# Both feed-forward products by Strassen's seven products, with the forms between them sent through HBM

## The chip, the cores and the metric

The kernel runs on one NeuronCore of one Trainium2 chip. Five engines take part: TensorE (PE, matmuls into the eight banks of PSUM), VectorE (DVE), ScalarE (ACT), GpSimd (POOL, here an issuer of DMAs and of a few memsets), and SyncE (SP, an issuer of DMAs). The metric is the device time of one execution in microseconds, the median over the runs. Lower is better.

## What is computed

A first block (attention with a stick-breaking weight, chunkwise retention, a gated merge) gives x. A second block mixes tokens with gated linear attention and sliding-window attention, and then has a feed-forward part. Only this last part is touched. Cut to what matters, with x of 1024 tokens by 1024 columns in float32:

```python
D_FF = 4 * D_MODEL                      # 4096
h = rmsnorm(x, norm_ff_w)               # 1024 x 1024
a = jnp.square(jax.nn.relu(h @ w_ff1))  # 1024 x 4096
x = x + a @ w_ff2                       # 1024 x 1024
out = rmsnorm(x, final_norm_w)
```

Every operand of a matmul is held as two fp32r values, hi and lo = value - hi, and a product is the sum of three: hi*hi, hi*lo and lo*hi. A block of 256 weight columns on all 1024 tokens and 1024 inner rows is thus 8 x 3 matmuls of 512 columns for each of its four outputs of 128 x 512.

## The kernel before

The stages follow one another: 30 projection blocks of the first layer, attention, retention, merge, the second layer's mixers, its output product (four blocks, L7), the norm before the feed-forward (`n3`), and then the feed-forward itself.

**Feed-forward.** It runs in four turns (`ff_turn`: line 1298 on ACT, 1889 on DVE, 2500 on PE; the last three PE turns, and the first three of ACT and DVE, are hardware loops). In each turn PE first makes four blocks of 256 hidden columns from `A_hi`, `A_lo` (line 450: weights stationary, 512 tokens moving), then four blocks of 256 output columns from the hidden values `F_hi`, `F_lo` of this turn (line 444: tokens stationary, 256 weight columns moving, two such strips in one bank). All go through `gemm` (line 431), which uses banks 0 to 3 in turn and waits for `kept[j]` before bank j is written again. SP loads one megabyte of weights for each block (`load_block`, 417) into one of two slots; ACT rounds it to hi (`split_hi`, line 425), DVE subtracts to get lo (`split_lo`, line 429). Hidden outputs are taken by ACT (relu, line 1305, then square into `F_hi`, line 1307) and by DVE (square again, 1896, minus hi, 1898). Outputs of the second product are added by DVE to the residual `X1` in place (line 1906), which stays in SBUF. The last norm (ACT 1319 to 1323, `final_scale` 1911 on DVE) goes by tiles of 128 tokens while the last block is made, and SP stores each tile.

**The norm before it.** `LateNorm` (313) is laid over the last block of the output product: for each of eight tiles of 128 tokens ACT makes the statistics (336 to 340), DVE scales (364), PE transposes eight squares into two banks (395), ACT rounds to `A_hi` (345), DVE makes `A_lo` (369). `pe_between` (398) puts the transpositions between outputs: tiles 6 and 7 come after output 0 of the first hidden block, and transposition t waits for the lo of tile t-1.

**The projections already have the seven products.** `product` (1948) makes one of seven products of a 2 x 2 split: 4 inner rows x 3 matmuls of 512 columns, in bank (7n + o) % 4; its bank is written again four products later, after `product_read` (576). DVE makes the four weight sums (`proj_sums`, 1349, 1355 to 1361), the lo parts (`proj_lo`, 1363, 1369) and seven additions that put the products together (`with_product`, 1413, 1415); ACT keeps product 0 (934) and rounds seven weight parts (865, 872). POOL stores four results of 256 KB in each block (756). The moving operands are parts of `A_hi`/`A_lo` for three products and of packed token sums `T_hi`/`T_lo` for four.

The order on every engine is the order of the program, written out by hand; there is no planner. DMAs of SP and POOL are issued in order in each queue, and a wait there holds back all that is behind it.

Of the kernel before, what the change touches and what calls it, by code (L numbers as in the profile page):

```python
# [5 lines left out]
SEQ, DM = 1024, 1024  # L6
# [59 lines left out]
def build(nc, x, norm_gain, w_in, b_merge, sb_q_gain, sb_k_gain, ret_out_gain, w_branch_sb, w_branch_ret, w_out,  # L66
# [152 lines left out]
    pos[0] = work_at  # L219
    F_hi = work("f_hi", [P, KT, SEQ], f32r)  # L220
    F_lo = work("f_lo", [P, KT, SEQ], f32r)
    FS = [work(f"fs{u}", [P, HALF]) for u in range(2)]

    YB = [at(f"yb{u}", [P, DM], off=a_at + u * DM * 4) for u in range(4)]
    GF = at("gf", [P, DM], off=a_at + 4 * DM * 4)

    ctx = ExitStack()
    with ctx:
# [18 lines left out]
        NPROJ = 30  # L247
        proj_d = nc.dram_tensor("projections", (NPROJ, P, 2 * SEQ), f32, kind="Internal").ap()
# [64 lines left out]
        class LateNorm:  # L313
# [3 lines left out]
            def __init__(self, name, eps, n, gain_at, meta_in=None):  # L317
# [4 lines left out]
            def parts(self, t):  # L322
# [4 lines left out]
                return (X1[:, t, :], XS[t % 4][:, :], stats[:, 16 + t:17 + t],  # L327
# [33 lines left out]
            def dve_scale(self, dve, t):  # L361
                src, scr, st, _, _ = self.parts(t)
                dve.wait_ge(self.rstd, self.m + t + 1)
                dve.scalar_tensor_tensor(scr, src, st, G1[0:src.shape[0], :], ALU.mult, ALU.mult).then_inc(self.scaled, 1)
# [38 lines left out]

        def level_keep(dve, p, v):
# [26 lines left out]
        def gemm(pe, n, s, hi, lo, rows_out, between=None, before=None, banks=range(4)):  # L431
# [72 lines left out]
        n2 = LateNorm("norm2", 1e-5, L6 - 1, 16, meta_in)  # L504
        n3 = LateNorm("norm3", 1e-5, L8 - 1, 32)
# [12 lines left out]
        f_hi = sem("hidden_hi")  # L518
# [71 lines left out]
        def tile_free(eng, n, j):  # L590
# [3 lines left out]
            elif before:  # L594
                eng.wait_ge(c_stored[out_tile(n, j)], stores_before(n, j))

        @block.sync
        def _(sp):
# [119 lines left out]
            with sp.Fori(0, 2) as i:  # L718
                for s in range(2):
                    load_block(sp, L7 + 2 * i + s, s, w7_d[:, :, ds(i * (2 * BC) + s * BC, BC)])  # L720
            f1_d = w_ff1_2[0].rearrange("(k p) c -> p k c", p=P)
            f2_d = w_ff2_2[0].rearrange("(g k p) c -> p g k c", p=P, k=KT)
            with sp.Fori(0, 4) as i:
                for s in range(4):
                    load_block(sp, L8 + 8 * i + s, s % 2, f1_d[:, :, ds(i * (4 * BC) + s * BC, BC)])
                for s in range(4):
                    load_block(sp, L8 + 8 * i + 4 + s, s % 2, f2_d[:, ds(i, 1), :, s * BC:(s + 1) * BC].rearrange("p g k c -> p (g k) c"))
# [1816 lines left out]
```

## Time and profile before

| | us |
|---|---|
| median of 3 runs (2843.64 to 2852.22) | 2848.79 |
| the profiled execution, its own time | 2846.42 |
| its span, first to last instruction | 2844.9 |
| PE busy in the span | 2714.9 |
| DVE / ACT busy | 1382.2 / 970.4 |
| POOL / mean DMA rate | 139.8 / 74 GB/s |
| mean granted TensorE clock | 0.973 of full |

Busy time of PE counts modelled ends of overlapping matmuls; the distance from one start to the next is the better measure of its pace. Idle time of an engine that nobody waits for costs nothing. The page's "L" numbers are lines of the kernel before.

### The profile page before, as it was taken

What the parts mean: (1) busy time and instruction counts of PE and PEld (TensorE: products, weight loads), DVE (VectorE), ACT (ScalarE), POOL (GpSimd) and SP (SyncE); (2) the same over time, 40 slices, a digit from 0 to 9 for tenths busy, and PEclk for the clock granted to TensorE, in tenths of its full rate; (3) what the DMA queues carried; (4) which work ended last, traced back from release to release, by engine and by line L of the source; (5) the groups of instructions that cost most, each with busy time, mean ns of one, the idle gap of its engine ahead of it and who ended that gap; (6) DMA issues with size and microseconds to landing.
All of it is one profiled execution on the core that took longest, in us unless ns stands there. A gap on an engine that the chain in (4) does not pass through costs nothing.

```text
span 2844.9 us, 36583 instructions
## 1 busy us (share of the span) xinstructions
PE 2714.9 (95%) x15024; PEld 2293.6 (81%) x15024; DVE 1382.2 (49%) x1818; ACT 970.4 (34%) x1587; POOL 139.8 (5%) x231
## 2 busy tenths in 40 slices
PE   5999999999999999999999899999999999999998
PEld 4777888887777778788897668877888989989888
DVE  7665556555565553656434571377343232232223
ACT  6444222334666553124123341243233021120221
POOL 0001111110000001000110000000100000000000
PEclk7999999999999999999999899898999999999999
DMA  2223333323202206342322001100221111111112
GB/s 98 89 92 112 97 115 97 111 102 120 82 28 82 74 26 228 106 163 67 114 86 104 16 1 45 45 16 1 89 64 49 45 45 45 46 45 46 52 53 82
DMA packets 129133, 211.67 MB, mean 74 GB/s; under 512 B 6205, under 2 KB 107242, under 8 KB 124762
## 3 DMA queue, kind: packets, MB, share of 16 engines
q1 hardware_dynamic: 110186, 147.16, 15.6%
q0 software_dynamic: 18800, 62.38, 6.2%
q8 instruction: 113, 1.85, 0.3%
q14 instruction: 34, 0.28, 0.0%
HBM read 163.38 MB, written 46.14 MB: 74 GB/s over the span
## 4 chain that ended last, share of the span: by engine, by line
PE 87%; DVE 5%; ACT 3%; issue 2%; DVEq 1%; ACTq 1%; DMA 1%; SPq 0%; POOL 0%; POOLq 0%
PE ps L450 23%; PE ps L1956 20%; PE ps L444 20%; PE ps L2055 4%; PE ps L2039 2%; PE ps L2012 2%; PE ps L2338 2%; PE ps L2405 2%; PE ps L2420 1%; PE ps L2218 1%; PE ps L1966 1%; PE ps L2023 1%; PE ps L2190 1%; DVEq L1492 1%; PE ps L2118 1%
## 5 line engine op out<-in xcount | busy, mean ns | idle before, releaser
L425 ACT ACTIVATE w_hi<-w_raw 128x2048 fp32r<-128x2048 f32 x60 | 114.8, 1914 | 554.5 <-DMA w_raw<-in_w_ff 363.1
L450 PE MATMUL ps<-a_hi,w_hi 128*128 128x512 f32 x736 | 295.4, 401 | 4.8 <-issue 3.5
L450 PE MATMUL ps<-a_lo,w_hi 128*128 128x512 f32 x736 | 292.9, 398 | 0.0
L450 PE MATMUL ps<-a_hi,w_lo 128*128 128x512 f32 x736 | 290.7, 395 | 0.0
L444 PE MATMUL ps<-w_lo,f_hi 128*128 128x256 f32 x1024 | 289.8, 283 | 0.0
L444 PE MATMUL ps<-w_hi,f_hi 128*128 128x256 f32 x1024 | 289.8, 283 | 0.0
L444 PE MATMUL ps<-w_hi,f_lo 128*128 128x256 f32 x1024 | 289.8, 283 | 0.0
L429 DVE TENSOR_TENSOR w_lo<-w_raw,w_hi 128x2048 fp32r<-128x2048 f32 x60 | 137.4, 2291 | 311.8 <-ACT w_hi L425 311.8
L1415 DVE TENSOR_TENSOR proj_out<-ps,proj_out 128x512 f32<-128x512 f32 x210 | 142.0, 689 | 237.7 <-PE ps L1956 237.7
L1956 PE MATMUL ps<-t_hi,pw_hi 128*128 128x512 f32 x480 | 196.4, 409 | 3.8 <-DVE t_lo L1389 3.8
L444 PEld LDWEIGHTS ps<-w_hi,f_hi 128*128 128x128 f32 x1024 | 196.6, 192 | 0.2
L444 PEld LDWEIGHTS ps<-w_lo,f_hi 128*128 128x128 f32 x1024 | 196.6, 192 | 0.2
L444 PEld LDWEIGHTS ps<-w_hi,f_lo 128*128 128x128 f32 x1024 | 196.6, 192 | 0.0
L1956 PE MATMUL ps<-t_lo,pw_hi 128*128 128x512 f32 x480 | 188.1, 392 | 0.0
L444 PE MATMUL ps<-w_hi,a_hi 128*128 128x256 f32 x640 | 181.5, 284 | 5.1 <-DVE a_lo L1815 5.1
L444 PE MATMUL ps<-w_lo,a_hi 128*128 128x256 f32 x640 | 181.4, 283 | 0.0
L444 PE MATMUL ps<-w_hi,a_lo 128*128 128x256 f32 x640 | 181.4, 283 | 0.0
L450 PEld LDWEIGHTS ps<-a_hi,w_hi 128*128 128x128 f32 x736 | 139.5, 190 | 40.9 <-issue 6.8
L450 PEld LDWEIGHTS ps<-a_lo,w_hi 128*128 128x128 f32 x736 | 139.2, 189 | 33.8 <-issue 2.2
L450 PEld LDWEIGHTS ps<-a_hi,w_lo 128*128 128x128 f32 x736 | 139.6, 190 | 31.8
L1956 PE MATMUL ps<-a_hi,pw_hi 128*128 128x512 f32 x360 | 150.9, 419 | 3.5 <-DVE a_lo L1347 3.5
L1956 PE MATMUL ps<-a_lo,pw_hi 128*128 128x512 f32 x360 | 144.1, 400 | 0.0
(365 smaller groups left out, 5688.0 us busy)
## 6 DMA issues: line engine op xcount, KB each, us to landing
w_raw<-in_w_ff SPq DMA_DIRECT2D x32, 1024.0 KB, 5.2
pw_raw<-in_w_in SPq DMA_DIRECT2D x30, 1024.0 KB, 5.4
projections<-proj_out POOLq DMA_DIRECT2D x88, 256.0 KB, 3.4
w_raw<-in_w_in SPq DMA_DIRECT2D x20, 1024.0 KB, 5.2
projections<-proj_sq POOLq DMA_DIRECT2D x32, 256.0 KB, 2.7
w_raw<-in_w_out SPq DMA_DIRECT2D x8, 1024.0 KB, 5.0
x_in<-in_x SPq DMA_DIRECT2D x8, 512.0 KB, 5.4
q<-projections SPq DMA_DIRECT2D x4, 1024.0 KB, 4.8
```

Of the source, the lines that this page charges most:

```text
L425: act.activation(W_hi[s][:, :, :], W_raw[s][:, :, :], ACT.Copy).then_inc(w_hi, 1)
L429: dve.tensor_tensor(W_lo[s][:, :, :], W_raw[s][:, :, :], W_hi[s][:, :, :].bitcast(f32), ALU.subtract).then_inc(w_lo, 1)
L444: last = pe.matmul(bank[banks[j]][:, r * BC:(r + 1) * BC], a[:, k, t:t + P], w[s][:, k, :], start=(k == 0 and g == 0), stop=(k == KT - 1 a ...
L450: last = pe.matmul(bank[banks[j]][:, :], w[s][:, k, ct * P:(ct + 1) * P], a[:, k, t0 + th * HALF:t0 + (th + 1) * HALF], start=(k == 0 and ...
L1415: return dve.tensor_tensor(PC[out_tile(n, j)][:, :], product_bank(n, o), src, ALU.add)
L1492: dve.drain()
L1956: last = pe.matmul(product_bank(n, o), w, a[:, k0 + k, t], start=(k == 0 and g == 0), stop=(k == 3 and g == 2))
L2012: pe.matmul(z, Q[:, c, qt * P:(qt + 1) * P], K[:, c, h:e], start=True, stop=(e < w))
L2039: last = pe.matmul(bank[2][:, lo:2 * P], V[:, kb, c * P:(c + 1) * P], WT[c][:, kb, lo:2 * P], start=(kb == 0), stop=(kb == qt))
L2055: last = pe.matmul(bank[3], w[b][:, k, ct * P:(ct + 1) * P], a[:, k, META + th * HALF:META + (th + 1) * HALF], start=(r == 0), stop=(r == ...
L2338: last = pe.matmul(bank[7][:, 0:2 * P], a, b, start=(m == 0), stop=(m == len(ops) - 1))
L2405: last = pe.matmul(bank[2 * (U % 3) + t // 4][:, (t % 4) * P:(t % 4 + 1) * P], a, b, start=True, stop=True)
```

## The change

**First product.** Hidden block 0 stays a plain `gemm` with its own weight tiles (`FD_hi`, the second projection weight slot). Hidden blocks 1 to 15 become blocks `NPROJ` to `NPROJ + 14` of the projection scheme: seven products each, with `proj_sums`, `proj_lo`, `with_product` as they are. The token sums are new: ACT copies the first half of the tokens out once more (`F_FIRST`), DVE makes the sums, partly inside the norm, from PSUM (`TokenSumNorm`).

**Between the products.** ACT applies relu and square in place to the four tiles of a block. DVE makes three sums and one difference of them (`hidden_sums`, one block later). POOL stores the seven forms (`a11 a22 a12 s1 s3 s2 s4`, 256 KB each) in HBM, 28 MB in all. `X1` is stored too (4 MB) and its space reused.

**Second product.** Four groups of 1024 hidden rows, seven products in each, 28 products. A product reads one form (1 MB, `hidden_form` on SP, ring of three) and one weight form made from quarters of 1 MB (`weight_quarter`, 16 in all, ring of five). It is four row outputs of 128 tokens x 512 columns: 4 x 4 x 3 matmuls of 512 columns, in one half of PSUM, the other half being read. For each, ACT rounds both forms (128 x 2048 each), DVE makes a weight sum in four of seven (`weight_sum`), both lo parts, and adds the four banks to an accumulator (`keep_product`). The residual is loaded into three accumulators and one spare quarter. Late products gather the accumulators into `Y`, tokens 512 to 1023 first, and the last norm runs on these tiles in the order 4 5 6 7 0 1 2 3.

The core of the diff:

```diff
+        class TokenSumNorm(LateNorm):
+            def act_hi(self, act, t):
...
+                last = act.activation(A_hi[:, :, c], turned, ACT.Copy)
+                if t < 4:
+                    act.activation(F_FIRST[0][:, :, t * P:(t + 1) * P], turned[:, 0:4, :], ACT.Copy)
+                    last = act.activation(F_FIRST[1][:, :, t * P:(t + 1) * P], turned[:, 4:8, :], ACT.Copy)
+                last.then_inc(self.hi, 1)
+            def dve_lo(self, dve, t):
...
+                last = dve.tensor_tensor(A_lo[:, :, c], turned, A_hi[:, :, c].bitcast(f32), ALU.subtract)
+                if t >= 4:
...
+                    dve.tensor_tensor(FT_raw[1][:, :, q], turned[:, 0:4, :], F_FIRST[0][:, :, q], ALU.subtract)
+                    dve.drain()
+                    last = dve.tensor_tensor(FT_raw[2][:, :, q], turned[:, 4:8, :], FT_raw[1][:, :, q], ALU.subtract)
+                last.then_inc(self.lo, 1)
 # SP
+            for g in range(1, 26):
+                hidden_form(g + 2)
+                for q in range(16):
+                    if max(1, 7 * (q // 4) + R_USED[q % 4] - 2) == g and q + 5 < 16:
+                        weight_quarter(q + 5)
 # POOL
+            for b in range(NHID + 1):
+                n = F0 + b
+                for v, (name, j) in enumerate((("a11", 0), ("a22", 1), ("a12", 2)) if b else (("a11", 0), ("a12", 2), (None, 3), ("a22", 1))):
+                    if name:
+                        pool.wait_ge(first_ok, HID0 + 4 * b + v + 1)
+                        store_form(b, name, hidden_tile(n, j))
+                for v, (name, src) in enumerate((("s1", NB[0]), ("s3", hidden_tile(n, 3)), ("s2", NB[1]), ("s4", NB[2]))):
+                    pool.wait_ge(head_scaled, HSUM0 + 4 * b + v + 1)
+                    store_form(b, name, src)
 # ACT
+            for g in range(28):
+                if g < 27:
+                    hidden_hi(g + 1)
+                if g < 26:
+                    weight_hi(g + 2)
 # DVE, second product
+            for g in range(28):
+                weight_sum(g + 2)
+                if g < 27:
+                    weight_lo(g + 1)
+                    hidden_lo(g + 1)
+                if g == 0:
+                    hidden_sums(LASTF)
+                else:
+                    keep_product(g - 1)
...
+                elif g == 24:
...
+                    gather(6, 1)
+                    gather(3, 5)
...
+                    gather(3, 6)
+                    dve.tensor_tensor(ACC[5], ACC[5], QUARTER[1][:, :, :], ALU.add)
+                elif g == 26:
+                    gather(7, 6)
...
+                    for t in range(4):
+                        dve.tensor_tensor(Y[4 + t][:, 0:HALF], ACC[4][:, t, :], ACC[7][:, t, :], ALU.add)
+                        dve.tensor_tensor(Y[4 + t][:, HALF:DM], ACC[5][:, t, :], ACC[7][:, t, :], ALU.add).then_inc(y_ready, 1)
...
+            keep_product(27)
 # PE, second product
+            for g in range(28):
+                u = g % 3
+                pe.wait_ge(w_lo, WH0 + g + 1)
+                pe.wait_ge(t_dve, HL0 + g + 1)
+                for t in range(4):
+                    if g >= 2:
+                        pe.wait_ge(kept[t], K0 + g - 1)
+                    tok = slice(t * P, (t + 1) * P)
+                    for k in range(4):
+                        for v, (a, w) in enumerate(((HF_hi, WS_hi), (HF_hi, WS_lo), (HF_lo, WS_hi))):
+                            last = pe.matmul(bank[4 * ((g + 1) % 2) + t], a[u][:, k, tok], w[u][:, k, :],
+                                             start=(k == 0 and v == 0), stop=(k == 3 and v == 2))
+                    last.then_inc(gp_done, 1)
```

`weight_lo(g)` and `hidden_lo(g)` wait for ACT's hi of product g. `weight_sum(g)` and both `hi` wait until product g-3 is done, whose slots they take. `hidden_form(g)` waits for product g-3 as well, and at the first product of a group for the stores of its four blocks.

## Rows read from the trace of the kernel before

**Rows 1.** The page, parts 1 and 4: engines, and the chain that ended last.

```profile
PE 2714.9 (95%) x15024; PEld 2293.6 (81%) x15024; DVE 1382.2 (49%) x1818; ACT 970.4 (34%) x1587; POOL 139.8 (5%) x231
...
PE 87%; DVE 5%; ACT 3%; issue 2%; DVEq 1%; ACTq 1%; DMA 1%; SPq 0%; POOL 0%; POOLq 0%
```

**Rows 2.** Windows: one stretch of projections, the feed-forward, the end.

```profile
core 0: us, PE busy (x) PEld busy (x) DVE busy (x) ACT busy (x) POOL busy (x), PEclk, DMA share, GB/s
361.00:438.00 77.00, 77.00 (x337) 63.00 (x336) 46.05 (x72) 17.87 (x32) 8.65 (x16) 1.00 0.34 108
2105.20:2835.60 730.40, 726.87 (x4624) 658.69 (x4623) 212.46 (x232) 151.53 (x195) 0.00 (x0) 1.00 0.16 49
2835.60:2844.90 9.30, 0.00 (x0) 0.00 (x0) 5.47 (x5) 3.00 (x8) 0.00 (x0) 0.67 0.56 226
```

**Rows 3.** Lines of PE, 2104 to 2845 us.

```profile
L444 PE MATMUL ps<-w_hi,f_hi 128*128 128x256 f32 x1024 | 289.8, 283 | 0.0
...
L450 PE MATMUL ps<-a_hi,w_hi 128*128 128x512 f32 x512 | 201.3, 393 | 3.5 <-issue 3.5
```

**Rows 4.** Timeline of PE: transpositions before the first matmul, and the last matmul.

```profile
2103.24 1.96 PE L395 MATMUL ps<-ident,xs 128*128 128x128 f32 x16
...
2835.32 0.28 PE L444 MATMUL ps<-w_hi,f_lo 128*128 128x256 f32 x1
```

**Rows 5.** Timeline of DVE, 2130 to 2330 us: two outputs of each product.

```profile
2147.43 0.69 DVE L1896 TENSOR_TENSOR fs<-nb 128x512 f32<-128x512 f32 x1 [4.10 <-ACT f_hi L1307]
...
2152.99 0.69 DVE L1896 TENSOR_TENSOR fs<-nb 128x512 f32<-128x512 f32 x1 [4.10 <-ACT f_hi L1307]
...
2213.41 0.69 DVE L1906 TENSOR_TENSOR x<-ps,x 128x512 f32<-128x512 f32 x1 [5.07 <-PE ps L444]
2219.18 0.69 DVE L1906 TENSOR_TENSOR x<-ps,x 128x512 f32<-128x512 f32 x1 [5.07 <-PE ps L444]
```

**Rows 6.** Timeline of POOL, 250 to 420 us: last stores of two plain blocks.

```profile
361.07 0.54 POOL L756 DMA_DIRECT2D projections<-proj_out  x1 [1.35 <-DVE proj_out L1415]
...
380.36 0.54 POOL L756 DMA_DIRECT2D projections<-proj_out  x1 [1.35 <-DVE proj_out L1415]
```

**Rows 7.** The page, part 5, and lines of DVE and ACT, 2104 to 2845 us.

```profile
L1415 DVE TENSOR_TENSOR proj_out<-ps,proj_out 128x512 f32<-128x512 f32 x210 | 142.0, 689 | 237.7 <-PE ps L1956 237.7
...
L429 DVE TENSOR_TENSOR w_lo<-w_raw,w_hi 128x2048 fp32r<-128x2048 f32 x31 | 71.1, 2292 | 165.8 <-ACT w_hi L425 165.8
...
L1915 DVE SCALAR_TENSOR_TENSOR yb<-x,stats,gf 128x1024 f32<-128x1024 f32 x8 | 9.8, 1278 | 0.0
...
L425 ACT ACTIVATE w_hi<-w_raw 128x2048 fp32r<-128x2048 f32 x31 | 59.4, 1915 | 363.1 <-DMA w_raw<-in_w_ff 363.1
...
L1305 ACT ACTIVATE nb<-ps 128x512 f32<-128x512 f32 x64 | 37.9, 593 | 179.1 <-PE ps L450 179.0
L1319 ACT ACTIVATE yb<-x 128x1024 f32<-128x1024 f32 x8 | 8.4, 1051 | 29.7 <-DVE x L1906 29.7
```

**Rows 8.** Timeline of ACT and of DVE, 2060 to 2130 us: the norm.

```profile
2097.13 1.06 ACT L336 ACTIVATE xs<-x 128x1024 f32<-128x1024 f32 x1 [2.39 <-DVE x L1671]
...
2109.13 2.35 DVE L369 TENSOR_TENSOR a_lo<-ps,a_hi 128x1024 fp32r<-128x1024 f32 x2
```

**Rows 9.** DMA issues by line, KB each, median us to landing.

```profile
w_raw<-in_w_ff SPq DMA_DIRECT2D x32, 1024.0 KB, 5.2
...
projections<-proj_out POOLq DMA_DIRECT2D x88, 256.0 KB, 3.4
...
rk<-projections SPq DMA_DIRECT2D x4, 1024.0 KB, 10.8
...
x_saved<-x POOLq DMA_DIRECT2D x1, 4096.0 KB, 13.2
...
out<-yb SPq DMA_DIRECT2D x8, 512.0 KB, 2.8
```

**Rows 10.** Timeline of DVE, 2788 to 2846 us: the last scalings.

```profile
2836.24 4.86 DVE L1915 SCALAR_TENSOR_TENSOR yb<-x,stats,gf 128x1024 f32<-128x1024 f32 x4
```

More of the change, by code:

```diff
@@ L217, in build @@
     KEM = work("kem", [P, META])
[L219 to L225, printed above, removed]
+    NS = [at(f"norm3_scaled{u}", [P, DM], off=o) for u, o in enumerate((region + 120 * KB, region + 124 * KB, nb_at, nb_at + 4 * KB))]
+    G3 = at("g3", [P, DM], off=region + 128 * KB)
@@ L1311, in _ @@
[L1311 to L1323 removed]
+            split_hi(act, L7 + 1, 1)
@@ new lines, in _, with first_hidden_hi, first_hidden @@
+            proj_hi_first(NPROJ)
+            split_hi(act, L7 + 2, 0)
+            proj_hi_sums(NPROJ)
+            split_hi(act, L7 + 3, 1)
+            def first_hidden_hi():
+                act.wait_ge(w_loaded[0], 8 * L8 + 16)
+                act.activation(FD_hi[:, :, :], PWR[1][:, :, :], ACT.Copy).then_inc(w_hi, 1)
+            n3.act(act, first_hidden_hi)
+            def first_hidden(j, t):
+                act.wait_ge(gp_done, done(L8, j))
+                act.activation(t[:, :], bank[j], ACT.Relu).then_inc(kept[j], 1)
+                act.drain()
+                act.activation(t[:, :], t[:, :], ACT.Square).then_inc(first_ok, 1)
@@ new lines, in _ @@
+            for n in range(NPROJ, NPROJ + NHID):
+                if n > NPROJ:
+                    hidden(n - 1, 3)
+                act.wait_ge(product_done, 7 * n + 1)
+                hidden_free(act, n, 0)
+                act.activation(out_ap(n, 0), product_bank(n, 0), ACT.Copy).then_inc(by_act, 1)
+                if n < LASTF:
+                    proj_hi_first(n + 1)
+                hidden(n, 0)
+                if n < LASTF:
+                    proj_hi_sums(n + 1)
+                else:
+                    hidden_hi(0)
+                    weight_hi(0)
+                hidden(n, 1)
+                hidden(n, 2)
@@ L2516, in _ @@
-            ff_turn(0, True)
-            with pe.Fori(1, 4) as i:
-                ff_turn(i, False)
+            gemm(pe, L8, 0, A_hi, A_lo, False, between=lambda j: j == 0 and n3.pe_between(pe, 4),
+                 before=lambda j: after_norm(n3, j), W_hi=[FD_hi], W_lo=[PWL[1]])
+            for n in range(NPROJ, NPROJ + NHID):
+                pe.wait_ge(pw_lo, 2 * n + 1)
+                for o in range(7):
+                    if o == 1:
+                        pe.wait_ge(pw_lo, 2 * n + 2)
+                    if n == NPROJ:
+                        if o < 4:
+                            pe.wait_ge(kept[(7 * n + o) % 4], kept_by(L8))
+                        if o in (1, 3, 4, 5):
+                            pe.wait_ge(t_dve, {1: 11, 3: 12, 4: 13, 5: 14}[o])
+                    product(n, o)
```

454 lines of the change are left out of this document (351 added, 103 removed).

## The prediction

> **What bounds the kernel now.** I read the page first: the chain that ended last is 87% PE, while DVE is busy for 49% of the span and ACT for 34% [rows 1]. That is an average over stages, so the question is whether it holds where the change is. The windows say so: in the 730.4 us from the first matmul of the feed-forward to its last [rows 2, 4], PE is busy for 726.9, DVE for 212.5, ACT for 151.5, the DMA engines for 16%, at a granted clock of 1.00 (the 2.4 GHz level). The lines of PE show where the missing 3.5 us are: two stops put down to "issue" at a first matmul, one at each of two loop turns, and no wait for another engine [rows 3]. So every matmul taken out here shortens the kernel, as long as the others keep up.
>
> The pace of PE is read from the outputs as DVE takes them, not from busy time. A hidden output is 24 matmuls of 512 columns and comes every 5.56 us (2147.43 to 2152.99), 231.7 ns each. An output of the second product is 48 of 256 columns and comes every 5.77 us [rows 5], 240 ns for 512 columns. There are 64 of either kind: 355.8 + 369.3 = 725.1 us, with the stops 3.5 and the last 16 transpositions 2.0 [rows 4]: 730.6, against 730.4 in the window. The account closes.
>
> The third pace is that of the seven products already in the kernel. The last stores of two plain blocks lie 19.29 us apart (361.07 to 380.36) [rows 6]; a block is 84 matmuls, so 229.6 ns each, and I found no wait of PE in that stage.
>
> **The first product.** Block 0 stays as it is: 4 x 5.56 = 22.2 us. The other 15 take 15 x 19.29 = 289.4. Against 355.8 that is 44.2 us less. Does the rest keep up? In a plain block DVE is busy 46.05 us in 77.0, which is four blocks, so 11.5 per block [rows 2]; `hidden_sums` adds four of 0.69 [rows 7], together 14.3 of 19.29. ACT has 17.87 / 4 = 4.5, and eight of about 0.6 (relu and square of four tiles) make it 9.3. The new sums stand behind `with_product(n,0,2)`. What they push back, in order: product 3's sum, three lo parts, products 4 and 5's sums, four lo parts. The next block needs the first lo parts at its start and bank 3 back four products later; following the order with these durations, each comes over 3 us early. SP's queue keeps its one load per block. POOL's has seven stores in place of four, about 0.55 us of issue each [rows 6], landing in 3.4 us [rows 9]; a tile is written again one or two blocks later. `s1` holds up what is behind it in that queue, the next block's `a11` among it, until DVE has made the sums, but that `a11` is later anyway. Cost beyond PE: nothing, covered by 5 us of free DVE time per block; if that cover went, a block would grow by what is over it.
>
> **The norm before it.** ACT makes two more copies for each of four token tiles, eight x 0.59 [rows 7] = 4.7 us, and in each pair of tiles it was idle 2.39 us [rows 8], so part disappears. DVE makes two sums for each of the four later tiles, eight x 0.69 = 5.5 us with four drains, behind each `a_lo` (a pair of them took 2.35 [rows 8]). Transpositions 6 and 7 wait for the lo of tiles 4 and 5, and the second hidden output waits for the transpositions. No row shows this mix. From below: 0, all of it in idle time. From above: 10.2, all of it exposed. Walking the order, tiles 2 and 3 come 1.5 us late, the add of output 3 about 3.7, and transposition 7 about 6.4; I take 6, near the upper end because this chain has no slack where PE waits for it already. The six whole-tensor operations for the token sums (2.29 each, 13.8 us) follow under the 22.2 us of block 0, and the saves of `X1` (4 MB in 13.2 us [rows 9]) under the norm and that block: nothing for either.
>
> **The second product.** 28 products x 48 = 1344 matmuls of 512 columns. At the pace of the seven products, 229.6 ns, that is 11.02 us per product and 308.6 in all, 60.7 less than 369.3. At 231.7 it would be 311.4. I take the first, because most of these operands lie packed, as in that stage. The Trainium skill, "TensorE: Matmul & The Clock Gate", section "Back-to-back issue gap", gives about N/2.4 + 2.5 ns for N columns, which makes two matmuls of 256 columns only 1% dearer than one of 512, where the rows above show 5% (240 against 229.6). By its figures, as an estimate, the wider rows would bring 4 us where I count 15, and the sum would be some 11 us longer; the trace differs from it, and I go by the rows.
>
> DVE per product: lo of the hidden form and of the weight form, 2.29 each, a weight sum of 2.29 in four of seven, and four additions of 0.69 [rows 7]: 9.6 with a sum, 7.3 without, under 11.02. ACT: two of 1.92. What DVE releases is early: both lo parts stand ahead of the four additions, so they are done some 7 us into a product and are needed at its end. SP has 1 MB per product and 16 quarters of 1 MB over 28, 1.57 MB in 11.02 us = 143 GB/s, against 108 that the projections move [rows 2] and some 318 for the save of 4 MB in 13.2 us [rows 9]. A load lands in 5.2 us and is asked for two products ahead. Nothing again, up to the point where DVE has 1.4 us left.
>
> Two places have less room. At the first products ACT and DVE still have the last hidden block: sum of product 6, weight sum, lo, lo is 7.6 us of the 11.02, with ACT's relu, square and two roundings partly in series. Bounds: 0, and one exposed set of two roundings and two subtractions, 8.4; by walking the order it just fits, and I take 1. At product 24 DVE has 7.3 + 4 x 2.29 = 16.5 us and falls 5 behind, then less; PE's operands still come first, and I take nothing.
>
> **The tail.** Before: 9.3 us from the last matmul's end to the end of the span [rows 2]. After: DVE is behind from the gathers and the first four scalings, so it begins the last four additions only when PE is done. Then four additions 2.8, one statistic about 1.6 (1.05 and small ones [rows 7]), four scalings of 1.28, the last store 2.8 [rows 9]: 12.3, less overlaps, 12.0, so 2.7 more. Before it was 0.69, then four scalings in 4.86 us [rows 10] and the store. Bounds 0 and 6.
>
> **Sum.** PE's stretch after: 22.2 + 289.4 + 308.6 + 2.0 + 6 + 1 = 629.2, against 730.4: 101.2 less. Tail 2.7 more: 98.5 less. The profiled execution took 2846.42 (span 2844.9), 2.4 under the median of the runs, so the forecast is **2748 us**. Its own range is 2738 (norm, bubble and tail all hidden) to 2758.
>
> **Rivals.**
> - *VectorE sets the pace of the second product.* Sixteen products have 9.6 us of work and seven or more waits. If these cost 0.4 us each over the busy time, such a product takes 12.5 us: 16 x 1.5 = 24 us more, 2772. For it: DVE is the nearest engine to PE. Against it: in the blocks of seven products DVE waits as often and PE does not slow.
> - *The wide rows do not run faster.* If a row product of 512 columns keeps the 240 ns of today's row product, 1344 x 0.0108 = 14.5 us come back: 2762. For it: no row here has tokens stationary and 512 columns moving. Against it: 512 columns run at 229.6 to 231.7 with weights stationary.
> - *Slower: the forms' way through HBM becomes the bound of the second product.* Its place is SP's queue there. One load of a projection, 1 MB, had a median of 10.8 us to landing [rows 9]; at that rate 1.57 MB take 17.0 us per product, 28 x 6.0 = 167 us more, 2915. It decides from 14.5 us per product (98.5 / 28 = 3.5 over 11.02). For it: 56 MB more traffic. Against it: those loads were asked for together with others, and the ring here is two products deep.
>
> **Chances.** Forecast 0.74, VectorE 0.13, wide rows 0.08, HBM 0.05, of which 0.01 ends near no change. A difference within 0.3%, 8.5 us, is about what a measurement of this kernel cannot tell from none. So faster 0.94, same 0.01, slower 0.05. The range is 2738 to 2774: it takes in the first three cases and leaves out the last.
>
> **What would show it.** Right: hidden blocks 19.3 us apart, row products 11.0 apart, PE's stretch near 629, no DVE or DMA among the releasers of PE between. A start from 2105 to the second hidden output longer by 6 than now bears out the norm. VectorE as bound would show as PE waiting for `ws_lo` or `kept` in products with a sum; the HBM case as ACT waiting for `hidden_raw` with PE behind. The forecast is wrong if products of the second kind are over 11.6 us apart, or if the clock in them falls below 1.00.

## The result, and the profile after

The changed kernel takes 2753.22 us (median of 4 runs, 2752.22 to 2756.20); the kernel before, on the same chip, 2846.76 (4 runs, 2843.64 to 2852.22). The ratio is 0.9671, with an interval of 0.9653 to 0.9689: faster by 93.5 us. The forecast was 2748, the range 2738 to 2774. The profiled execution took 2752.22 us, its span is 2750.7.

The page of the changed kernel, parts 1, 4 and 6, against [rows 1] and [rows 9]. The last line is of DMA issues: count, size, median us to landing.

```profile
PE 2609.2 (95%) x13116; PEld 2142.8 (78%) x13116; DVE 1656.8 (60%) x2141; ACT 1096.0 (40%) x1744; POOL 206.7 (8%) x351
...
PE 82%; DVE 7%; ACT 4%; issue 2%; DVEq 2%; DMA 1%; ACTq 1%; POOL 0%; SPq 0%; POOLq 0%
...
hidden_raw<-hidden_forms SPq DMA_DIRECT2D x28, 1024.0 KB, 4.8
```

PE has 1908 matmuls fewer and is busy for 105.7 us less. DVE is now busy for 60% of the span (49 before), and the chain is 82% PE where it was 87%, so other work ends waits in more places. The windows show which. In the lines below 2105 to 2422 is the first product, 2422 to 2736.8 the second with its first products apart, the last stretch the tail; they answer to the second and third line of [rows 2].

```profile
core 0: us, PE busy (x) PEld busy (x) DVE busy (x) ACT busy (x) POOL busy (x), PEclk, DMA share, GB/s
2105.00:2422.00 317.00, 314.49 (x1381) 257.09 (x1381) 231.33 (x341) 155.73 (x255) 58.64 (x108) 1.00 0.47 154
2440.00:2454.80 14.80, 14.80 (x67) 12.08 (x65) 8.91 (x7) 0.12 (x1) 0.74 (x1) 1.00 1.01 379
2454.80:2459.70 4.90, 0.24 (x2) 0.07 (x1) 3.08 (x3) 3.59 (x2) 0.00 (x0) 0.86 1.03 404
2459.70:2473.40 13.70, 13.70 (x48) 10.96 (x49) 13.70 (x13) 5.64 (x3) 0.00 (x0) 0.80 0.35 135
2473.40:2736.80 263.40, 263.40 (x1153) 216.12 (x1151) 204.75 (x169) 90.37 (x60) 0.75 (x1) 1.00 0.36 131
2736.80:2750.70 13.90, 0.08 (x1) 0.00 (x0) 8.13 (x9) 6.11 (x16) 0.00 (x0) 0.67 0.61 243
```

The hidden blocks and 263 of the 315 us of row products run at the full clock with PE busy throughout (the 2.5 us missing in the first line are in the norm). The other lines are the story of this case: 14.8 us in which the DMA engines are full (share 1.01, 379 GB/s), then 4.9 in which PE stands, then 13.7 at a granted clock of 0.80.

The pace of the hidden blocks, on the timeline of DVE: the first addition of one block and of the next, as the stores in [rows 6] showed it for the projections.

```profile
2389.18 0.69 DVE L1665 TENSOR_TENSOR proj_out<-ps,proj_out 128x512 f32<-128x512 f32 x1 [4.85 <-PE ps L2342]
...
2408.47 0.69 DVE L1665 TENSOR_TENSOR proj_out<-ps,nb 128x512 f32<-128x512 f32 x1 [4.85 <-PE ps L2342]
```

19.29 us, the same as before to the hundredth. The timeline of PE at row products 3, 6, 7 and 9, and the last matmul:

```profile
2459.66 0.77 PE L2911 MATMUL ps<-a_hi,hidden_hi 128*128 128x512 f32 x1 [4.66 <-DVE gated_first L2255]
2460.22 0.63 PE L2911 MATMUL ps<-a_lo,hidden_hi 128*128 128x512 f32 x1
2460.65 0.63 PE L2911 MATMUL ps<-a_hi,hidden_lo 128*128 128x512 f32 x1
...
2495.17 0.40 PE L2911 MATMUL ps<-a_hi,hidden_hi 128*128 128x512 f32 x1
...
2506.32 0.40 PE L2911 MATMUL ps<-ws_hi,hidden_hi 128*128 128x512 f32 x1
...
2528.09 0.40 PE L2911 MATMUL ps<-a_hi,hidden_hi 128*128 128x512 f32 x1
...
2736.49 0.39 PE L2911 MATMUL ps<-a_hi,hidden_lo 128*128 128x512 f32 x1
```

Product 6 runs from 2495.17 to 2506.32, 11.15 us; products 7 and 8 to 2528.09, 10.88 each. But for the stop and the product behind it, all 28 follow this pattern: every third product (its weight form in a slot of the `A` buffer, names `a_hi`, `a_lo`) takes 11.14, the others (packed slots) 10.88. Products 1 and 2 with the stop in front of product 3 took 26.6 in place of 21.8; product 3 took 13.74, for it begins with matmuls 0.43 us apart, half the pace of the 0.23 that follow: the 1.2 GHz level after 4.8 us without a matmul.

All waits of PE for another engine from the norm to the end (us in total, times, longest):

```profile
PE ps L2911 <- DVE gated_first L2255: 4.7, 1, 4.7
PE ps L419 <- DVE a_lo L444: 4.3, 4, 2.3
PE ps L419 <- DVE ft_raw L451: 2.5, 2, 1.4
```

### The profile page after: what moved, and what is told of

It is laid out like the page before. It is cut to its first block, busy times and chain, and to the rows that moved or that the text cites. A ratio compares the mean times of both kernels' runs of the same rounds, so it can differ in the third digit from the quotient of the medians.

```text
span 2750.7 us, 33350 instructions
## 1 busy us (share of the span) xinstructions
PE 2609.2 (95%) x13116; PEld 2142.8 (78%) x13116; DVE 1656.8 (60%) x2141; ACT 1096.0 (40%) x1744; POOL 206.7 (8%) x351
## 3 DMA queue, kind: packets, MB, share of 16 engines
q0 software_dynamic: 29936, 100.14, 10.2%
## 4 chain that ended last, share of the span: by engine, by line
PE 82%; DVE 7%; ACT 4%; issue 2%; DVEq 2%; DMA 1%; ACTq 1%; POOL 0%; SPq 0%; POOLq 0%
PE ps L2342 31%; PE ps L500 11%; PE ps L2911 8%; PE ps L494 7%; PE ps L2441 4%; PE ps L2791 2%; PE ps L2425 2%; PE ps L2724 2%; PE ps L2398 2%; PE ps L2806 2%; PE ps L2604 1%; PE ps L2352 1%; DVEq L1742 1%; PE ps L2409 1%; PE ps L2576 1%
## 5 line engine op out<-in xcount | busy, mean ns | idle before, releaser
L2342 PE MATMUL ps<-a_hi,pw_lo 128*128 128x512 f32 x360 | 142.3, 395 | 0.0
L494 PEld LDWEIGHTS ps<-w_hi,a_hi 128*128 128x128 f32 x640 | 122.3, 191 | 5.6 <-ACT gv L1425 5.5
L2342 PEld LDWEIGHTS ps<-a_hi,pw_hi 128*128 128x128 f32 x540 | 101.9, 189 | 31.2 <-DVE a_lo L1597 3.9
L494 PEld LDWEIGHTS ps<-w_hi,a_lo 128*128 128x128 f32 x640 | 122.5, 191 | 0.0
L2342 PEld LDWEIGHTS ps<-a_lo,pw_hi 128*128 128x128 f32 x540 | 101.8, 189 | 26.2 <-issue 3.8
L494 PEld LDWEIGHTS ps<-w_lo,a_hi 128*128 128x128 f32 x640 | 122.2, 191 | 0.0
L1619 DVE TENSOR_TENSOR pw_lo<-pw_raw,pw_hi 128x512 fp32r<-128x512 f32 x180 | 115.5, 683 | 0.1
L2911 PE MATMUL ps<-ws_hi,hidden_hi 128*128 128x512 f32 x288 | 112.1, 389 | 0.0
L2911 PE MATMUL ps<-ws_lo,hidden_hi 128*128 128x512 f32 x288 | 112.1, 389 | 0.0
L2911 PE MATMUL ps<-ws_hi,hidden_lo 128*128 128x512 f32 x288 | 112.0, 389 | 0.0
```

The lines of the kernel that those rows point to most:

```text
L494: last = pe.matmul(bank[banks[j]][:, r * BC:(r + 1) * BC], a[:, k, t:t + P], w[s][:, k, :], start=(k == 0 and g == 0), stop=(k == KT - 1 a ...
L1619: last = dve.tensor_tensor(lo_part(s, q), raw_part(s, q), PWH[s][:, q, :, :].bitcast(f32), ALU.subtract)
L2342: last = pe.matmul(product_bank(n, o), w, a[:, k0 + k, t], start=(k == 0 and g == 0), stop=(k == 3 and g == 2))
L2911: last = pe.matmul(bank[4 * ((g + 1) % 2) + t], a[u][:, k, tok], w[u][:, k, :], start=(k == 0 and v == 0), stop=(k == 3 and v == 2))
```

## Where the 93.5 us come from, and the 4.3 that are missing

Cut at events that both traces have, in us; the prediction's terms are summed in the same way.

| part | before | predicted | after |
|---|---|---|---|
| first transposition of the norm to the first row product | | 338.5 | 337.8 |
| row products | | 309.6 | 314.8 |
| both together | 749.3 | 648.1 | 652.7 |
| last matmul to the end of the span | 9.3 | 12.0 | 13.9 |

Against the forecast that is -0.7 + 5.2 + 1.9 = 6.4; the stages ahead of the norm, which the change doesn't touch, were 2.2 us shorter in this profile (the norm begins at 2084.11, before at 2086.30), and the span comes out 4.3 above the 2746.4 forecast for it (the parts, rounded, give 4.2). In the profiles of the runs below this start lies between 2080.8 and 2093.3 with the same code ahead of it, so the parts tell more than one whole time.

The row products are the larger miss, and it has two halves of opposite sign: the steady pace sums to 10 x 11.14 + 18 x 10.88 = 307.2, 1.4 under the 308.6 forecast; the stop and the slow stretch behind it add 7.6 where "I take 1". The chain of waits through that stop (start, us, what):

```profile
2432.55 0.61 DVE nb L2176
...
2433.62 0.54 POOL hidden_forms L1009
...
2435.62 3.63 DMA hidden_forms<-nb
...
2439.26 0.03 SPq L880
...
2439.32 0.38 SPq L863
...
2439.75 14.90 DMA hidden_raw<-hidden_forms
...
2458.83 0.69 DVE gated_first L2255
...
2459.66 10.44 PE ps L2911 x33
```

Read upwards from the last line: PE waits for the accumulation of product 1's bank (`gated_first`, L2255), which in DVE's order stands behind `hidden_lo` of product 3. That waits for ACT, ACT for form 3 from HBM. Form 3 landed 14.90 us after its issue, where the median is 4.8. And it was issued late, 6.7 us into product 1 (2433.06 to 2439.75): SP stood at line 880, waiting for the stores of the last two hidden blocks, which POOL issues from 2433.62 on, once DVE has made the sums, and the last of which lands at 2439.25. That wait belongs to the fifth quarter, which is loaded over the buffers that these stores read; form 3 needs none of it, since its own group was stored some 200 us earlier. Two theories follow. **Order:** form 3 stands behind a wait that isn't its own. **Burst:** in the same 15 us POOL issues three residual loads of 1 MB (2438.48 to 2440.7), SP three quarters and two forms (2439.32 to 2448.94): 8 MB, and the engines are full.

The tail, on the timeline of DVE:

```profile
2730.27 2.47 DVE L2251 TENSOR_TENSOR y<-ps,gated_first 128x512 f32<-128x512 f32 x4
2732.66 4.86 DVE L2268 SCALAR_TENSOR_TENSOR y<-y,stats,gf 128x1024 f32<-128x1024 f32 x4
2737.45 1.28 DVE L2251 TENSOR_TENSOR y<-ps,acc 128x512 f32<-128x512 f32 x2
2739.88 1.28 DVE L2268 SCALAR_TENSOR_TENSOR y<-y,stats,gf 128x1024 f32<-128x1024 f32 x1 [1.16 <-ACT stats L1573]
...
2745.32 1.28 DVE L2268 SCALAR_TENSOR_TENSOR y<-y,stats,gf 128x1024 f32<-128x1024 f32 x1 [0.51 <-ACT stats L1573]
```

DVE has no gap over 0.1 us from 2682 to 2738.7. PE ends at 2736.8, DVE begins with product 27 at 2737.45, behind 4.86 us of scalings, so every addition stands on the path, the last three each with a scaling after it, and two of the scalings wait for ACT's statistics. The last scaling ends at 2746.60, 9.8 us after PE; from there to the end of the span it is 4.1 us, the last store and what follows it.

## Experiments

Each edit is made to the changed kernel. "Row products" is the time from the first to the last of them, 314.8 in the changed kernel, and "tail" from there to the end of the span, 13.9.

**1. Order alone.** SP asks for form 3 ahead of the wait for the stores.

```diff
+            hidden_form(3)
             for name in FORMS:
                 for b in range(NHID - 1, NHID + 1):
                     sp.wait_ge(*form_stored(b, name))
...
             for g in range(1, 26):
-                hidden_form(g + 2)
+                if g > 1:
+                    hidden_form(g + 2)
```

> The changed kernel, but SP asks for the form of product 3 as soon as product 0 is done, ahead of its wait for the stores of the last two hidden blocks. In the changed kernel PE stands 4.8 us before product 3, and the granted clock then is at its lower level for part of that product (13.74 us in place of 11.14). Theory: the stop comes from SP's queue, in which the request for this form stands behind that wait and is then asked for in one burst with others (14.9 us to landing). Then the form is asked for at about 2433.5 in place of 2439.8, the stop and the slow stretch go, and the kernel takes 7.4 us less, about 2746 against 2753 (PE's stretch about 645 in place of 652.7). Rival 1: the stop comes from DVE, which is late from the last hidden block (sums, two subtractions in series with ACT); then the stop stays within 1 us and so does the time. Rival 2: it is the rate of the DMA engines in the burst (residual, quarters and forms together); then it shrinks to about half, 3 us less in all.

Measured: 2749.35 us (4 runs), ratio to before 0.9654 [0.9627, 0.9682]; against the changed kernel the intervals overlap, so the parts decide: row products 308.8, 6.0 less, and the stop in front of product 3 is gone. What is left is a stop of 1.2 us one product later. Its chain:

```profile
2446.99 16.19 DMA hidden_raw<-hidden_forms
...
2463.21 1.93 ACT hidden_hi L1534
...
2467.37 0.70 DVE a_plain L2257
...
2468.20 1.85 PE ps L2913 x7
```

Form 4 now stands where form 3 stood, behind the wait: asked at 2446.99, and 16.19 us on the way. So the order was a cause, but it moved the long landing to a product with more room, it didn't remove it.

**2. Burst alone.** The order stays; POOL holds the residual back until product 2 is done.

```diff
             pool.wait_ge(product_done, 7 * LASTF + 7)
+            pool.wait_ge(gp_done, G0 + 4 * 2 + 4)
             residual(ACC[4], 1, 0, late_gain)
```

> The changed kernel, but POOL asks for the three megabytes of the residual only after product 2. Rival 2 of the run before (the DMA engines are at their limit in the burst): form 3 lands some 5 us sooner and the stop before product 3 falls from 4.8 to about 0. Theory (the order of SP's queue): form 3 is still asked for at about 2439.8; with a free road it would land in about 6 to 9 us in place of 14.9, so the stop may fall too, but the request stays late. The two are told apart with the run before: if that one removes the stop with the residual in place, the order is enough; if this one removes it as well, either is enough.

Measured: one run of 2750.59 us, span 2749.1, with a start 5.7 us later than in the changed kernel (the stages ahead). Row products 307.4, and PE waits for no other engine in them. Form 3 was still asked behind the same wait. So either half removes most of the stop, and holding back three of the eight megabytes removes all: form 3 then landed 7.1 us after its issue, and with that the late request is affordable. 307.4 is also the steady sum of 307.2, so nothing else in this product costs anything.

**3. Do wide rows run faster?** Each row product in two strips of 256 columns, as all row products of the kernel before.

```diff
-                    for k in range(4):
...
-                            last = pe.matmul(bank[4 * ((g + 1) % 2) + t], a[u][:, k, tok], w[u][:, k, :],
...
+                    for h in (slice(0, BC), slice(BC, HALF)):
+                        for k in range(4):
...
+                                last = pe.matmul(bank[4 * ((g + 1) % 2) + t][:, h], a[u][:, k, tok], w[u][:, k, h],
```

> The changed kernel with each row product of 512 columns of the second product made as two strips of 256 columns, one after the other, as the kernel before did. By the rows of the kernel before (240 ns for 512 columns in two halves) a product takes 48 x 0.240 = 11.54 us in place of 10.88 to 11.14, and the kernel 28 x 11.54 - 307.2 = 15.9 us more, 2769. By the page rule of the Trainium skill (TensorE: Matmul & The Clock Gate, Back-to-back issue gap), N/2.4 + 2.5 ns, as an estimate two halves cost 3.4 us more in all: 2757. If instead DVE set the pace of these products, nothing would change: 2753.

Measured: 2762.17 us (2761.16 to 2769.40, 4 runs), ratio 0.9707 [0.9682, 0.9732]. The timeline of PE at the starts of products 6, 7 and 9:

```profile
2496.10 0.28 PE L2912 MATMUL ps<-a_hi,hidden_hi 128*128 128x256 f32 x1
...
2507.47 0.28 PE L2912 MATMUL ps<-ws_hi,hidden_hi 128*128 128x256 f32 x1
...
2530.50 0.28 PE L2912 MATMUL ps<-a_hi,hidden_hi 128*128 128x256 f32 x1
```

11.37 for product 6 and 11.52 for 7 and 8, so a steady sum of 10 x 11.36 + 18 x 11.52 = 321.0, 13.8 us above 307.2. That is the forecast's account of the row width within about 2 us of 15.9, and "the wide rows do not run faster" falls. The kernel as a whole lost less, 9.0 us (row products 324.3 against 314.8): with slower products the stop in front of product 3 was 3.1 us and no slow stretch followed it, so it cost 3.3 in place of 7.6. Matmuls of 256 columns are 118.3 to 120.0 ns apart here. The estimate from the Trainium skill, "TensorE: Matmul & The Clock Gate", section "Back-to-back issue gap", was 3.4 us for this edit. The trace does not agree, neither in the difference nor in the levels (by the formula 109 and 216 ns, in the trace 118 to 120 and 227 to 232). The section calls this the gap of a single matmul by itself and gives about 131 ns for 512 columns in a stream with weight loads; the trace, which is such a stream, has 227 to 232 and agrees with neither.

**4. Has DVE the room that was claimed?** In 16 products one more operation of 2.29 us, a maximum of a tensor with itself.

```diff
             for g in range(28):
+                if 7 <= g < 23:
+                    idle = ACC[7 if 4 not in ((g - 1) % 7, (g - 2) % 7) else 1]
+                    dve.drain()
+                    dve.tensor_tensor(idle, idle, idle, ALU.max)
                 weight_sum(g + 2)
```

> The changed kernel with one more DVE operation of 128 x 2048 (a maximum of an accumulator with itself, 2.29 us) in each of sixteen products, 7 to 22, ahead of the weight sum. If PE sets the pace and DVE has 1.5 us or more left in each product, the sixteen times 2.2 us mostly vanish: DVE is over 11.1 us only in the ten products with a sum, by 0.3 to 0.5, and gets it back in the others; 0 to 4 us more in all. If DVE set the pace already, all of it shows: 16 x 2.2 = 35 us more.

Measured: 2752.74 us (one run); row products 314.4 against 314.8, and the only wait of PE is the old stop of 4.5. 36.6 us of work on DVE cost nothing, at up to 11.9 us of work in a product with a sum. The window over most of these products:

```profile
2500.00:2680.00 180.00, 180.00 (x789) 147.84 (x788) 171.29 (x124) 63.86 (x34) 0.75 (x1) 1.00 0.40 142
```

DVE is busy for 95% of it, PE for all of it. (That a product with over 11 us of DVE work fits is put down here to the products without a sum that follow before a bank is needed; no run takes that apart.) "VectorE sets the pace" falls.

**5. How far is the next bound?** The third of the three terms, lo times hi, is left out of every row product: 896 of 1344 matmuls run, so the output lacks that term.

```diff
-                        for v, (a, w) in enumerate(((HF_hi, WS_hi), (HF_hi, WS_lo), (HF_lo, WS_hi))):
+                        for v, (a, w) in enumerate(((HF_hi, WS_hi), (HF_hi, WS_lo))):
...
-                                             start=(k == 0 and v == 0), stop=(k == 3 and v == 2))
+                                             start=(k == 0 and v == 0), stop=(k == 3 and v == 1))
```

> The changed kernel without the third term of the second product (lo of the hidden form by hi of the weight form is left out, 448 of 1344 matmuls); all the rest of the work stays. PE then needs 32 x 0.227 to 0.232 = 7.3 us per product, DVE about 9.2 us with a weight sum and 7.0 without, 8.3 in the mean. If PE sets the pace of the changed kernel and DVE is next, the 28 products take about 28 x 8.3 = 232 to 245 us in place of 314.8, that is 70 to 80 us less (about 2675), and PE waits in them for DVE. If DVE or the loads of forms set the pace already, it stays near 315. If the clock's level falls at the new pauses, it is somewhere between.

Measured: 2702.75 us (one run), row products 253.3, outside the 232 to 245 expected. The waits of PE in them:

```profile
PE ps L2911 <- DVE gated_first L2255: 9.3, 1, 9.3
PE ps L2911 <- DVE gated_first L2253: 8.4, 1, 8.4
PE ps L2911 <- DVE a_plain L2257: 6.9, 4, 1.9
```

One stop (9.3) is the one known, longer as PE asks earlier; a second (8.4), in front of product 26, I did not expect. Most of the rest are waits for DVE in three of the four products of a group in which it makes a sum: these take 9.0 to 9.6 us. The fourth takes 7.6 and those without a sum 7.3 to 7.4, which is PE's own pace for 32 matmuls. The window over most of it, and DVE ahead of the second stop:

```profile
2425.00:2680.00 255.00, 216.35 (x906) 172.39 (x905) 240.98 (x195) 107.59 (x66) 6.26 (x10) 0.95 0.52 192
...
2650.86 2.29 DVE L2271 TENSOR_TENSOR a_plain<-a_plain 128x2048 f32<-128x2048 f32 x1
...
2664.24 2.47 DVE L2253 TENSOR_TENSOR gated_first<-gated_first,ps 128x512 f32<-128x512 f32 x4
```

DVE is busy 94% of the time. So the next bound is DVE: with these stops left out, seven products take 57.1 us (products 7 to 13), 8.2 each in the mean against 11.0 in the changed kernel, 2.8 us of room. That fits experiment 4, where 2.3 more fitted, and the forecast's step count, 9.6 with a sum and 7.3 without, within half a us. The second stop is DVE's too: from 2650.86 it makes the four whole-tensor operations of the gathers, 9.0 us, ahead of the operands and the bank that PE waits for, and from there to 2664.24 it isn't idle for more than 0.1 us at a time. The HBM way is not seen as a bound at this pace, apart from the burst.

**6. Is the norm's term real?** ACT makes its new copies twice, and DVE the first of its new sums twice (with their drains).

```diff
-                if t < 4:
+                for _ in range(2 if t < 4 else 0):
+                    act.drain()
                     act.activation(F_FIRST[0][:, :, t * P:(t + 1) * P], turned[:, 0:4, :], ACT.Copy)
...
-                    dve.tensor_tensor(FT_raw[1][:, :, q], turned[:, 0:4, :], F_FIRST[0][:, :, q], ALU.subtract)
+                    for _ in range(2):
+                        dve.tensor_tensor(FT_raw[1][:, :, q], turned[:, 0:4, :], F_FIRST[0][:, :, q], ALU.subtract)
+                        dve.drain()
```

> The changed kernel with the new work of the norm done twice: both ScalarE copies of tiles 0 to 3 again (2 x 0.55 us each tile), and the first VectorE sum of tiles 4 to 7 again (0.69 each), with the same results. In the changed kernel the way from the first transposition of the norm to the first row product is 337.8 us, 5.6 more than its parts had before. If that came from these operations standing in the chain ScalarE, VectorE, transposition, a second helping comes through as well: 4 x 1.1 = 4.4 on ScalarE and 2 x 0.7 = 1.4 on VectorE, 343 to 344. If the 5.6 us had another cause (the saves of the residual, the loads), it stays at 338.

Measured: 2758.81 us (one run); from the first transposition to the first row product 347.05, 9.2 more than 337.8, where about 6 was expected. The waits of PE:

```profile
PE ps L419 <- DVE a_lo L445: 7.4, 3, 3.6
PE ps L419 <- DVE ft_raw L454: 4.1, 2, 2.2
```

6.8 us of waits in the changed kernel (4.3 + 2.5), 11.5 now: 4.7 more for 5.8 us of added work and its drains. The other 4.5 us of the 9.2 are put down here to TensorE's clock, which in the changed kernel stays at 1.00 there (the longer intervals between PE's instructions in two stretches add up to nearly 5). The windows from the first transposition on, first of the changed kernel, then of this run:

```profile
2084.11:2130.00 45.89, 39.11 (x247) 34.12 (x246) 36.30 (x31) 29.98 (x51) 3.97 (x6) 1.00 0.24 91
...
2082.36:2133.00 50.64, 39.09 (x228) 34.49 (x227) 34.46 (x33) 30.53 (x55) 3.95 (x6) 0.87 0.21 82
```

So the chain has little slack, and the longer stops in it (3.6 and 2.2 us at the longest) are followed by stretches at the 1.2 GHz level. The kernel before waits 1.6 us for `a_lo` at this place; the 6.8 of the changed kernel are 5.2 more, which is nearly all of the 5.3 us that the norm grew by. An edit that takes the sums out of the chain was not run.

**7. The tail.** The scalings that stand ahead of product 27's additions go behind them, except two.

```diff
-                        if t:
-                            final_scale(3 + t)
+                        if t == 1:
+                            final_scale(0)
+                            final_scale(1)
...
-                    for v in range(4):
-                        final_scale(v)
             keep_product(27)
-            final_scale(7)
+            for v in range(2, 8):
+                final_scale(v)
```

> The changed kernel with DVE's last operations in another order: the additions of the last product come first as they are ready, the scalings of the first four tiles between and behind them. In the changed kernel the end of the span comes 13.9 us after PE's last matmul, and DVE has no idle time from the last gathers on. If the tail is long since DVE is behind with its work and makes four scalings first, it becomes about 12.2. If it is the chain statistic, scaling, store of the last tile alone, it stays at 13.9.

Measured: tail 12.6 in place of 13.9, with the other parts unchanged (337.8, 314.9); the one run took 2756.6 us, span 2755.1, since the norm began at 2089.8. The gain is 1.3 where 1.7 was expected. DVE's last scaling ends 8.0 us after PE in place of 9.8, 1.8 less: six scalings are 7.25 us without a gap behind the last addition, so DVE's own work now makes that part. But from there to the end of the span it is 4.5 us in place of 4.1: the last store took 4.0 us to land in place of 3.6.

**8. DVE's backlog given to GpSimd.** Experiment 7 and three of the whole-tensor sums of the last four products moved.

```diff
+            pool.wait_ge(post_done, POST + 1)
+            pool.tensor_tensor(ACC[3], ACC[3], ACC[5], ALU.add)
...
+            pool.tensor_tensor(ACC[5], ACC[5], QUARTER[1][:, :, :], ALU.add).then_inc(sv_zero, 1)
+            pool.wait_ge(post_done, POST + 2)
+            pool.tensor_tensor(ACC[3], ACC[3], ACC[6], ALU.add).then_inc(sv_zero, 1)
...
                 elif g == 24:
...
                     gather(6, 1)
-                    gather(3, 5)
...
-                    gather(3, 6)
-                    dve.tensor_tensor(ACC[5], ACC[5], QUARTER[1][:, :, :], ALU.add)
```

> The run before, and three of the accumulator sums of 128 x 2048 (6.9 us on DVE) made by GpSimd, which is idle there: accumulator 3 + 5, 5 + residual, 3 + 6. If the tail is DVE's backlog, it is worked off before PE's last matmul, and the tail becomes about 8 us in place of 13.9. Against it: no row shows how long GpSimd takes for such a sum; with more than some 9 us each it would be late for the last additions, and the tail stays at 12 or grows.

Measured: 2765.9 us (one run), span 2764.0. Tail 11.6, 1.0 less than in experiment 7, but row products 321.2, 6.3 more. Even the 1.0 isn't DVE's: its last scaling ends 8.0 us after PE as before, and it was the last store that landed sooner (3.1 us against 4.0). The timelines of GpSimd and then of DVE:

```profile
2700.01 4.62 POOL L1034 TENSOR_TENSOR acc<-acc,gated_first 128x2048 f32<-128x2048 f32 x1 [66.81 <-DVEq L2294]
...
2720.50 4.60 POOL L1039 TENSOR_TENSOR acc<-acc,a_plain 128x2048 f32<-128x2048 f32 x1 [9.24 <-DVEq L2300]
```

```profile
2697.40 2.48 DVE L2267 TENSOR_TENSOR gated_first<-ps,gated_first 128x512 f32<-128x512 f32 x4
2700.01 6.76 DVE L2282 TENSOR_TENSOR gated_first<-gated_first,a_plain 128x2048 f32<-128x2048 f32 x1
2706.70 6.71 DVE L2211 TENSOR_TENSOR ws_lo<-ws_raw,ws_hi 128x2048 fp32r<-128x2048 f32 x1
```

A sum takes 4.6 us on GpSimd (the one not shown 5.1), twice DVE's 2.29, and each of the three operations of DVE that run beside one takes 6.7: 4.4 us longer each. DVE was relieved of 6.9 us and lost 13.2; PE then waits for `a_plain` (3.6) and `gated_first` (1.3) where it had not, and after the first of these stops it runs some 1.5 us at the 1.2 GHz level. The Trainium skill, "SBUF — State Buffer", section "Who interferes with whom", says that a DVE instruction with two SBUF inputs contends with a GpSimd instruction that reads SBUF, and it calls such contention an exclusive lock. The trace agrees: if one waits for the whole of the other, 4.62 + 2.29 is 6.91, as an estimate, against 6.76. The additions at 2697.40, with one input in PSUM, ran before it; no row here shows such a one beside GpSimd's work.

**9. Both remedies together.** Experiments 2 and 7 in one kernel, and the changed kernel once more on the same chip.

> The changed kernel with both edits that shortened a part: the residual asked for after product 2, and the additions of the last product ahead of the scalings. If the two are independent, the stop before product 3 and its slow stretch (7.4 us) and 1.3 us of the tail go: from the first transposition of the norm to the end of the span 337.8 + 307.4 + 12.6 = 657.8 us in place of 666.6, and a median 8.7 us under that of the changed kernel on the same chip. If moving the residual only moves the stop to a later product or into the tail, it gives less than 3.

> The changed kernel as it is, for the comparison with the run before on the same chip: 0.967 of the kernel before; 337.8, 314.8 and 13.9 us in its three parts from the first transposition of the norm. The stages ahead, which are the same in all these kernels, differ by several us from profile to profile, so the parts tell more than the whole.

Measured, against 2849.72 us for the kernel before (9 runs): the changed kernel 2754.80 (2750.91 to 2758.32, 5 runs), ratio 0.9678 [0.9664, 0.9692]; with both edits 2744.25 (2740.12 to 2749.78, 5 runs), ratio 0.9643 [0.9627, 0.9658]. The intervals don't touch. Parts: 337.8 + 307.4 + 12.6 = 657.8, against 337.9 + 314.5 + 14.0 = 666.4. The parts account for 8.6 of the 10.5 us between the medians, which is what was expected; the rest is within the spread. The windows of the version with both, last hidden block to last matmul and tail:

```profile
2400.00:2725.00 325.00, 325.00 (x1422) 266.76 (x1421) 257.10 (x214) 122.55 (x90) 9.49 (x16) 1.00 0.46 167
2725.00:2738.60 13.60, 1.14 (x5) 0.57 (x4) 9.02 (x9) 3.74 (x12) 0.00 (x0) 0.72 0.77 309
```

325.00 of 325.00 us of PE at a clock of 1.00: nothing but PE's own work is left between the norm and the tail. It is the fastest run here of those that compute the whole, faster than both kernels.

## Why the prediction was right, and where it missed

- **The bound.** Right: PE's matmuls were the path, and 101.2 us were forecast for their stretch; 96.6 came (749.3 to 652.7).
- **Hidden blocks, 15 x 19.29.** Right to the hundredth, and no engine appears as releaser of PE in them. The pace of the seven products in the same kernel was the right row to take.
- **The norm, 6, between 0 and 10.2.** Right: 337.8 less 289.4, 22.2, 18.9 (first transposition to first matmul before, 2086.30 to 2105.2) and 2.0 is 5.3, and PE's waits for DVE there grew by 5.2 (1.6 to 6.8). Experiment 6 shows the chain to be about as tight as supposed.
- **Row products, 229.6 ns.** Right within 1.4 us: 226.7 ns in packed slots and 232 in the others. The reason given for the first ("most of these operands lie packed") agrees with that, though no run moves an operand to test it, and experiment 3 gives the 15 us of wide rows as 13.8. Here the sum went by the rows against the formula of the Trainium skill, "TensorE: Matmul & The Clock Gate", section "Back-to-back issue gap", and the rows were right; the forecast didn't say that this section means the formula for a matmul by itself.
- **VectorE as the bound, 0.13.** Fell, by experiment 4. The step count (9.6 with a sum) was right; the 0.4 us per wait were not there.
- **Wide rows no faster, 0.08.** Fell, by experiment 3.
- **HBM as the bound, 0.05.** Fell as a bound of the whole product: forms land in 4.8 us, row products are 10.9 to 11.1 apart. But its mechanism, a load that takes far longer since others were asked for with it, is what made the stop at product 3 (14.90 against the 10.8 that the rival took).
- **The step that failed** is "At the first products ... by walking the order it just fits, and I take 1", together with "A load lands in 5.2 us and is asked for two products ahead. Nothing again". The term was 7.6. The walk followed DVE and ACT at product 1, where it did fit (products 0, 1 and 2 run without a wait). It left out SP: form 3 stands behind a wait for stores that DVE's sums of the last hidden block release, so that it was asked 6.7 us into product 1 and not at its start; and it took a load at its median where three residual tensors and three quarters were asked for in the same 10 us. Both were in the diff. The bound of 8.4 held the size, though for another reason. Of the 7.6, 2.6 are the lower clock level after the stop, which no term had. By the forecast's own signs this was a miss: DVE stands once among the releasers of PE, and the clock in a row product fell below 1.00 (0.80 in product 3), which it had named as a sign of being wrong. It held for one product of 28, so the sum stayed near.
- **The tail, 12.0.** Mis-sized: 13.9. "Four additions 2.8, one statistic about 1.6 [...], four scalings of 1.28" is 9.5, and the last scaling does end 9.8 us after PE. The step that was off is "the last store 2.8": from the last scaling to the end of the span it is 4.1 (1.3 more), and the kernel before already had 3.8 there (2841.1 to 2844.9, by [rows 2] and [rows 10]). The 0.3 of "less overlaps" was not there.
- **Luck in the whole.** The misses from the norm on add up to 6.4 us; the median came out 5.2 above the forecast. 2.2 us of the miss went under in the stages ahead, which the change doesn't touch.
- **Small slips.** The chances of the three faster cases add up to 0.95 and not 0.94. The 143 GB/s are reckoned with a megabyte of 10^6 bytes, the 318 beside them with 1,048,576; in the latter both would be 149 and 318. Neither changes the forecast.

## What to carry to other kernels

Where a stage hands over to the next, follow every queue through the first two turns, the issuing engine's waits first: list which loads stand behind a wait that is not theirs, and sum the bytes that become issuable by the same event, for in the burst here a load took three times its median. A pace is best taken from the same instruction shape with the same kind of operand elsewhere in the trace; at two places here that came out within 0.5%. And before a backlog of VectorE is moved to GpSimd, look at whether both would read two tensors of SBUF at once.

## What the runs showed of the hardware that was not expected

- **A burst of loads.** A load of 1 MB that lands in 4.8 us (median of 28) took 14.90 and 16.19 us while the DMA engines were full, at 379 and 392 GB/s.
- **Where the moving operand lies.** With 512 columns, packed slots run at 226.7 ns per matmul and those in the `A` buffer at 232; with 256 columns it is the reverse, 120.0 against 118.3 (experiment 3). Why, no run here shows.
- **A short stop costs the clock as well.** 4.8 us without a matmul, and the next twelve came at the 1.2 GHz level, 0.43 us apart: 2.6 us on top. After the stop of 1.2 us in experiment 1 they were 0.23 apart at once, but for the first interval (0.31). The length of the stop alone doesn't settle it: behind 3.1 us in experiment 3 no matmul came at the lower level, behind 3.1 us in experiment 5 some did, from 1 us after the stop on.
- **GpSimd beside VectorE.** 2.29 us became 6.7 for additions and subtractions of 128 x 2048 in fp32 with both inputs in SBUF.
